# Mixer and passage of a three-stage decoder kernel on one core: conversions ahead of silus, squares and masks, and a norm that starts by token tile

## The chip, the cores and the metric

The kernel runs on one core of a Trainium2 chip. TensorE (PE in the profile) multiplies, VectorE (DVE) and ScalarE (ACT) work on the results, GpSimd (POOL) does a few small operations, and SyncE (SP) issues the loads. The metric is the device time of one execution in microseconds, as the median of several. Lower is better.

## The reference, cut to what matters

Two decoder blocks run one behind the other on 256 tokens of width 1024.

```python
x = x + _moba(_rmsnorm(x, norm_mix), w_qkv, w_o)           # attention, 16 heads
x = x + _conv_ffn(_rmsnorm(x, norm_ffn), w_up, conv, w_down)
x = _rmsnorm(x, norm_final)
h = layer_norm(concat([meta_tokens, x]), ln_emb_g, ln_emb_b)   # 16 + 256 tokens
mix = hybrid_mixer(h, ...)      # gated delta rule (4 heads) and stick-breaking attention
h = layer_norm(ALPHA * h + mix, ln1_g, ln1_b)
h = layer_norm(ALPHA * h + hierarchical_moe(h, ...), ln2_g, ln2_b)   # 32 experts
return h[:, 16:]
```

In the mixer q, k and v of the delta rule pass a causal convolution over 4 tokens and a silu; q and k are normalized by the root of their summed squares; the chunk matrices of q and k are masked, and a triangular system is solved in levels.

## The kernel before

Everything is written by hand in five instruction queues with semaphores; each engine works its own queue strictly in program order.

**Granules.** All weights but the experts' come in granules of 1 MB (128 x 2048), numbered through the program: 0 to 11 for q, k and v, 12 to 15 for the attention's output product (`G_WO` is 12), 16 to 48 for the FFN (`G_FFN` 16), 49 on for the mixer (`G_IN` 49: z, six of q, k and v in the order `DN_ORDER`, six for the other attention, eight gates, and so on). SP loads granule n into one of three buffers `raw` once granule n-3 has been converted (L558). `hi_part` (L744) lets ACT round it to the upper part `whi`, `lo_part` (L1173) lets DVE subtract that from the raw weights and store the rest as `wlo`; there are two slots of each, so granule n also waits for the product with granule n-2. Granules 14 and 48 have slots of their own (`OWN_SLOT`). PE then does three products for each tile (`split3`, L1733): upper by upper, upper by lower, lower by upper. A granule is 48 matmuls of 256 or 272 columns.

```python
def split3(dst, lh, ll, rh, rl, start, stop, **kw):
    pe.matmul(dst, lh, rh, start=start, stop=False, **kw)
    pe.matmul(dst, lh, rl, start=False, stop=False, **kw)
    return pe.matmul(dst, ll, rh, start=False, stop=stop, **kw)
```

**The passage from attention to FFN.** Granules 12 and 13 are multiplied head pair by head pair. Then PE does both token tiles of granule 14 and both of granule 15 (L1868 to L1871); DVE adds each result to the residual `X`; ACT sums the squares of each block of 256 columns (`ss_block`, L823); DVE adds these up, ACT takes the root, DVE takes the reciprocal and scales a tile of 1024 columns to `XN` (`norm_apply`, L1177). PE transposes the tile in 8 pieces (`norm_T`, L1726), ACT writes the upper part (`norm_hi`), DVE the lower (`norm_lo`), and the FFN's first granule waits for all of it. PE fills its waits with products of a row of zeros (`zeros`, L1878, 6, 7 and 7 of them); these also clear the four banks `PM` in which the FFN accumulates. The layer norm of the 16 meta tokens (`MT`, four DVE operations, L1253 to L1258) stands on DVE between granules 14 and 15; its result is first read after the FFN (L1927).

**The mixer's order** is a list `plan` (L208 on) that every engine walks through and takes its own part of: `whole(i)` or `half(i, f)` is PE's product with granule 49+i, and for ACT and DVE the conversion of the granule after it; `out_of(i)` takes the product out of PSUM (ACT a scaled copy, and for q, k and v DVE six tap operations, L1384); `silu`, `square`, `norm`, `G` (chunk matrix of k), `ktr` (k transposed), `QK`, `L0` (first triangular level: POOL masks it, L696, DVE subtracts it from the identity, L1502, PE transposes it, ACT copies it out) are steps of the delta rule. The steps named in `BANKED` share two PSUM banks in turn, in the order of the plan:

```python
TURN[st] = (len(TURN) % 2, len(TURN) // 2)
...
def vacant(eng, *st):
    b, k = TURN[st]
    if k:
        eng.wait_ge(pm_free[b], k)
    return PM[:, b, :]
```

So PE can begin a banked step only when the banked step two places ahead of it has been read out: a `norm` by ACT, a `G` by DVE.

## Time and profile before

| | |
|---|---|
| median of 3 runs | 917.32 us (916.73 to 917.66) |
| the profiled execution, its own time | 919.47 us |
| its span | 917.7 us |
| PE busy | 860.9 us, 94% of the span |
| DVE, ACT, POOL busy | 476.4, 370.0, 61.3 us |
| mean granted clock of TensorE | 0.982 |
| DMA | 193.48 MB, mean 211 GB/s |

The attention takes the first 118 us of the span, the passage 118 to 141, the FFN to 326, the mixer to about 605, the router and the experts the rest. Matmul ends in the profile are modelled: where matmuls follow one another, the distance of their starts tells the pace, not their length.

### The profile page before, as it was taken

How to read it: one execution, taken by the hardware profiler on the slowest of the kernel's cores; microseconds unless marked ns; L12 is line 12 of the kernel's file. 1: busy time of each engine (PE TensorE's matmuls, PEld its weight loads, DVE VectorE, ACT ScalarE, POOL GpSimd, SP SyncE). 2: the span in 40 equal slices, each digit the busy share in tenths (PEclk: the TensorE clock that was granted, in tenths of full speed). 3: DMA queues.
4: the chain of work that ended last, by engine and by line, in shares of the span. 5: the costliest groups of instructions: out<-in, count | busy, mean ns of one | idle time of the engine just before them, and what ended most of it. 6: DMA issues, size and time to landing. Idle time of an engine off the chain costs nothing.

```text
span 917.7 us, 15809 instructions
## 1 busy us (share of the span) xinstructions
PE 860.9 (94%) x6466; PEld 704.0 (77%) x6466; DVE 476.4 (52%) x802; ACT 370.0 (40%) x561; POOL 61.3 (7%) x88
## 2 busy tenths in 40 slices
PE   6999999999999999988999999999899999998882
PEld 6999978989989979988889999998555555544441
DVE  4555675776676786576433355685522322222225
ACT  4655544544555654664435444742211111111111
POOL 0200030000000000001211000003010000000000
PEclk9999997999999999999999999999999999999997
DMA  9854542555555543344122223499599999999991
GB/s 292 287 176 138 177 109 93 184 183 183 183 183 184 184 137 114 116 139 138 47 93 70 71 93 110 166 315 364 213 363 369 364 366 369 364 366 368 366 350 49
DMA packets 151152, 193.48 MB, mean 211 GB/s; under 512 B 4461, under 2 KB 135872, under 8 KB 150960
## 3 DMA queue, kind: packets, MB, share of 16 engines
q1 hardware_dynamic: 148816, 185.61, 60.9%
q0 software_dynamic: 1696, 4.59, 1.6%
q10 hardware_dynamic: 576, 2.36, 0.7%
q8 instruction: 48, 0.79, 0.4%
q14 instruction: 16, 0.13, 0.0%
HBM read 191.50 MB, written 1.05 MB: 210 GB/s over the span
## 4 chain that ended last, share of the span: by engine, by line
PE 74%; DVE 9%; DMA 5%; ACT 5%; SPq 4%; issue 3%; ACTq 0%; DVEq 0%
PE PG L1735 12%; PE PG L1737 12%; PE PG L1736 12%; PE PG L2209 10%; DMA expert_w<-in_expert_w_up 5%; PE PG L2227 4%; PE PM L2236 3%; DVE wlo L1175 3%; SPq L602 2%; PE PM L2063 2%; ACT whi L748 2%; PE PM L1735 2%; PE PM L1737 2%; PE PM L1736 2%; PE PM L2128 1%
## 5 line engine op out<-in xcount | busy, mean ns | idle before, releaser
L1735 PE MATMUL PG<-hT_hi,whi 128*128 128x256 f32 (+1 forms) x832 | 242.1, 291 | 4.6 <-DVE wlo L1175 4.6
L1737 PE MATMUL PG<-hT_hi,wlo 128*128 128x256 f32 (+1 forms) x832 | 237.7, 286 | 0.0
L1736 PE MATMUL PG<-hT_lo,whi 128*128 128x256 f32 (+1 forms) x832 | 237.5, 286 | 0.0
L1175 DVE TENSOR_TENSOR wlo<-raw,whi 128x2048 fp32r<-128x2048 f32 x77 | 177.3, 2302 | 96.4 <-ACT whi L748 96.2
L1735 PEld LDWEIGHTS PG<-hT_hi,whi 128*128 128x128 f32 x832 | 159.8, 192 | 10.5 <-issue 7.9
L1737 PEld LDWEIGHTS PG<-hT_hi,wlo 128*128 128x128 f32 x832 | 159.9, 192 | 0.0
L748 ACT ACTIVATE whi<-raw 128x2048 fp32r<-128x2048 f32 x77 | 146.9, 1908 | 31.4 <-PE PG L1737 26.5
L1736 PEld LDWEIGHTS PG<-hT_lo,whi 128*128 128x128 f32 x832 | 159.3, 191 | 0.1
L2209 PE MATMUL PG<-expert_w,xw 128*64 128x256 f32 x992 | 116.1, 383 | 10.5 <-DMA expert_w<-in_expert_w_up 9.9
L1675 DVE SCALAR_TENSOR_TENSOR y_lo<-PG,small,y_hi 128x512 fp32r<-128x512 f32 x32 | 24.0, 751 | 173.8 <-ACT y_hi L1122 173.8
L2209 PEld LDWEIGHTS PG<-expert_w,xw 128*64 128x64 f32 x992 | 69.4, 137 | 48.9 <-DMA expert_w<-in_expert_w_up 13.3
L2227 PE MATMUL PG<-expert_w,hid 128*64 128x512 f32 x256 | 61.9, 604 | 0.2 <-DMA expert_w<-in_expert_w_down 0.2
L1116 ACT ACTIVATE gusum<-PG 128x256 f32<-128x256 f32 x32 | 12.3, 384 | 119.5 <-PE PG L2209 119.5
L1122 ACT ACTIVATE y_hi<-PG,small 128x512 fp32r<-128x512 f32 x32 | 22.0, 687 | 86.1 <-PE PG L2227 86.1
L2227 PEld LDWEIGHTS PG<-expert_w,hid 128*64 128x64 f32 x256 | 15.6, 136 | 30.0 <-issue 28.2
L1735 PE MATMUL PG<-whi,hT_hi 128*128 128x256 f32 x128 | 36.4, 284 | 1.4 <-DVE hT_lo L1421 0.9
L1737 PE MATMUL PG<-whi,hT_lo 128*128 128x256 f32 x128 | 35.9, 281 | 0.0
L1736 PE MATMUL PG<-wlo,hT_hi 128*128 128x256 f32 x128 | 35.9, 281 | 0.0
L718 POOL COPY xw<-pair 128x512 f32 x31 | 19.1, 615 | 218.4 <-PE PG L2209 200.2
L1735 PE MATMUL PM<-whi,hid_hi 128*128 128x512 f32 x80 | 31.7, 396 | 0.2 <-DVE wlo L1175 0.2
L1793 PE MATMUL PG<-cst 128*128 128x128 f32 (+1 forms) x166 | 27.3, 321 | 4.8 <-DMA cst<-in_consts 4.8
L2236 PE MATMUL PM<-y_hi,hot 64*128 64x512 f32 x128 | 28.8, 444 | 2.9 <-DVE y_lo L1675 2.9
(432 smaller groups left out, 1322.1 us busy)
## 6 DMA issues: line engine op xcount, KB each, us to landing
expert_w<-in_expert_w_gate SPq DMA_DIRECT2D x64, 512.0 KB, 8.9
expert_w<-in_expert_w_up SPq DMA_DIRECT2D x64, 512.0 KB, 10.4
expert_w<-in_expert_w_down SPq DMA_DIRECT2D x32, 1024.0 KB, 10.6
raw<-in_ffn_w_up SPq DMA_DIRECT2D x22, 1024.0 KB, 5.0
raw<-in_w_in SPq DMA_DIRECT2D x22, 1024.0 KB, 5.2
raw<-in_moba_w_qkv SPq DMA_DIRECT2D x12, 1024.0 KB, 6.2
raw<-in_ffn_w_down SPq DMA_DIRECT2D x11, 1024.0 KB, 4.9
raw<-in_moba_w_o SPq DMA_DIRECT2D x4, 1024.0 KB, 5.2
```

The lines of the kernel that those rows point to most:

```text
L718: pool.tensor_copy(xw[i2][:, :, :], pair[:, :, bass.ds(at, WIN)]).then_inc(s_win, 1)
L748: act.activation(hi_of(n), raw[:, n % R, :], ACT.Copy).then_inc(s_hi, 1)
L1122: act.activation(y_hi[:, :], result, ACT.Copy, scale=slotw[i2]).then_inc(s_yhi, 1)
L1175: dve.tensor_tensor(lo_of(n), raw[:, n % R, :], hi_of(n).bitcast(F32), ALU.subtract).then_inc(s_lo, 1)
L1675: dve.scalar_tensor_tensor(y_lo[:, :], result, slotw[i2], y_hi[:, :].bitcast(F32), ALU.mult, ALU.subtract).then_inc(s_y, 1)
L1735: pe.matmul(dst, lh, rh, start=start, stop=False, **kw)
L1736: pe.matmul(dst, lh, rl, start=False, stop=False, **kw)
L1737: return pe.matmul(dst, ll, rh, start=False, stop=stop, **kw)
L1793: pe.matmul(PG[:, 3, 0:x.shape[1]], w, x, start=True, stop=True)
L2209: mm = pe.matmul(PG[WIN * h:WIN * h + WIN, i2, 0:EFF], x[:, KH * kind + k, :], w[:, k, EFF * h:EFF * h + EFF], start=kind + k == 0, stop=k ...
L2227: mm = pe.matmul(result[WIN * h:WIN * h + WIN, :], hid2[i2][:, f, :], w[:, f, 512 * h:512 * h + 512], start=f == 0, stop=f == 1)
L2236: mm = pe.matmul(PM[:, 2 * t + h, :], hot[i2][x, P * t:P * t + P], y[x, :], start=first and y is y_hi, stop=last and y is y_lo)
```

## The change

It has two parts that share nothing but the numbering of own slots.

**In the mixer's plan** the conversion of the next granule goes ahead of silus and squares. `silu` 0 and 1 stand ahead of `out_of(4)` (they read convolutions finished before), `square` 1 and `silu` 2 behind `whole(5)`, `silu_z` and `silu` 3 behind `whole(6)`, `square` 0 and `silu` 4 behind `whole(7)`. `G` 0, 1 and 2 stand ahead of the `norm` pairs that they followed. The subtraction from the identity is a step of its own, `U0`, behind `G` 2; before, DVE did it in `L0`.

**In the passage** granule 15 gets own slots, so it and the FFN's first two granules are converted earlier. PE does tile 0 of granules 14 and 15, then tile 1 of 14, half of tile 1 of 15, the transposes of tile 0, the other half, 12 warming matmuls with the identity, the transposes of tile 1 and 4 zero products. The scaling to `XN` and the waits for it go by halves of 512 columns; the FFN's first granule waits for its input by halves too. The meta tokens' norm goes behind the conversion of granule 17 on DVE.

```diff
-        OWN_SLOT = (14, 48)
+        OWN_SLOT = (14, 15, 48)
...
         whole(4)
-        out_of(4)
         plan_add("silu", 0)
         plan_add("silu", 1)
+        out_of(4)
+        whole(5)
         plan_add("square", 1)
-        whole(5)
+        plan_add("silu", 2)
         out_of(5)
-        plan_add("silu", 2)
         whole(6)
+        plan_add("silu_z")
+        plan_add("silu", 3)
         out_of(6)
-        plan_add("silu", 3)
+        whole(7)
         plan_add("square", 0)
-        plan_add("silu_z")
-        whole(7)
+        plan_add("silu", 4)
         out_of(7)
-        plan_add("silu", 4)
         half(8, 0)
...
         half(9, 0)
+        plan_add("G", 0)
         over("norm", chunks=(0, 1))
-        plan_add("G", 0)
         half(9, 1)
         out_of(9)
+        plan_add("G", 1)
         over("norm", chunks=(2, 3))
-        plan_add("G", 1)
         half(10, 0)
         plan_add("G", 2)
+        plan_add("U0")
         over("ktr", chunks=(0, 1))
...
+            hi_part(G_WO + 3)
...
+            hi_part(G_FFN)
+            for i in range(2):
+                for t in range(TT):
+                    ss_block(t, i, 256 * i, 256 * i + 256, evacs(G_WO + i))
+            hi_part(G_FFN + 1)
+            ss_block(0, 2, D // 2, D, evacs(G_WO + 1) + 2)
+            norm_sqrt(1, [0])
+            ss_block(1, 2, D // 2, 3 * D // 4, evacs(G_WO + 1) + 3)
+            norm_hi(1, [0])
+            ss_block(1, 3, 3 * D // 4, D, evacs(G_WO + 1) + 4)
+            norm_sqrt(1, [1])
+            norm_hi(1, [1])
...
+            dve.wait_ge(s_wo0, 1)
+            dve.tensor_tensor(X[:, 0, D // 2:D], X[:, 0, D // 2:D], PG[:, 2, :], ALU.add).then_inc(s_ev, 2)
+            scale_rows(0)
...
+            norm_lo(1, [0], [0])
+            scale_rows(1)
+            norm_lo(1, [0], [1])
+            norm_lo(1, [1])
...
+            last_rows(G_WO + 2, PG[:, 2, 0:256], 0, 0, KD)
+            last_rows(G_WO + 3, PG[:, 2, 256:512], 0, 0, KD).then_inc(s_wo0, 1)
+            last_rows(G_WO + 2, PM[:, 0, 0:256], 1, 0, KD).then_inc(s_gran, 1)
+            last_rows(G_WO + 3, PG[:, 3, 0:256], 1, 0, KD // 2)
+            pe.wait_ge(s_ev, evacs(G_WO + 1))
+            norm_T(1, 0)
+            last_rows(G_WO + 3, PG[:, 3, 0:256], 1, KD // 2, KD).then_inc(s_gran, 1)
...
+            keep_warm(12, con("ident"), con("ident"), PM[:, 3, :])
+            norm_T(1, 1)
...
+            for b in range(4):
+                pe.matmul(PM[:, b, :], zero[0:1, 0:P], zero[0:1, 0:512], start=True, stop=True)
...
-                features(n, 0, hT_hi, hT_lo, slice(0, SEQ), it)
+                features(n, 0, hT_hi, hT_lo, slice(0, SEQ), it, halves=(s_xlo, 7, 8) if first else None)
```

What it makes of the queues, at the three places that the prediction speaks of. (Lines of the changed file are some ten higher: L750 is `hi_part`, L1174 `lo_part`, L1745 to L1747 `split3`.)

ACT in the mixer, from the product with granule 53 on (`dnT<-PG` copies a product out, `dnT<-dnT` is a silu, `sqb<-dnT` a square, `whi<-raw` the next granule's conversion). Before:

```order
L945 ACTIVATE dnT<-PG,cols 128x272 [waits s_gran]
L945 ACTIVATE dnT<-PG,cols 128x272
L961 ACT_TABLE_LOAD
L961 ACTIVATE dnT<-dnT 128x544 [waits s_ev] x2
L969 ACTIVATE sqb<-dnT 128x1088 [waits s_dnsilu]
L748 ACTIVATE whi<-raw 128x2048 [waits s_gran,landed1]
```

Now:

```order
L960 ACT_TABLE_LOAD
L960 ACTIVATE dnT<-dnT 128x544 [waits s_ev] x2
L944 ACTIVATE dnT<-PG,cols 128x272 [waits s_gran]
L944 ACTIVATE dnT<-PG,cols 128x272
L750 ACTIVATE whi<-raw 128x2048 [waits s_gran,landed1]
L968 ACTIVATE sqb<-dnT 128x1088 [waits s_dnsilu]
L960 ACTIVATE dnT<-dnT 128x544 [waits s_ev]
```

The table load and two silus moved ahead of the copies, the square behind the conversion.

PE in the mixer, between the two halves of granule 58 (`PM<-dnT` is `G` 0, `PM<-sqb,cst` the two `norm` matmuls; pm_free0 and pm_free1 are the two banks). Before:

```order
L1990 MATMUL PM<-sqb,cst 128x272 [waits pm_free0,s_sq]
L1990 MATMUL PM<-sqb,cst 128x272 [waits pm_free1,s_sq]
L2015 MATMUL PM<-dnT 128x128 [waits pm_free0,s_l2]
L2015 MATMUL PM<-dnT 128x128 x3
L1735 MATMUL PG<-hT_hi,whi 128x256 [waits s_lo,s_ev]
```

Now:

```order
L2033 MATMUL PM<-dnT 128x128 [waits pm_free0,s_l2]
L2033 MATMUL PM<-dnT 128x128 x3
L2008 MATMUL PM<-sqb,cst 128x272 [waits pm_free1,s_sq]
L2008 MATMUL PM<-sqb,cst 128x272 [waits pm_free0,s_sq]
L1745 MATMUL PG<-hT_hi,whi 128x256 [waits s_lo,s_ev]
```

`G` 0 moved ahead of both norm matmuls, and the second of them now takes the bank that `G` 0 held. On DVE the conversion of granule 59 stands ahead of the reading of `G` 0 (`dA<-PM`) in both. Before:

```order
L1175 TENSOR_TENSOR wlo<-raw,whi 128x2048 [waits s_hi]
L1435 SCALAR_TENSOR_TENSOR dnT<-dnT,sqb 128x272 [waits pm_free0]
L1435 SCALAR_TENSOR_TENSOR dnT<-dnT,sqb 128x272 [waits pm_free1]
L1477 TENSOR_TENSOR dA<-PM,small 128x512 [waits pm_full0]
L1479 TENSOR_TENSOR dA<-dA,dE 128x512 [waits s_E,s_dve]
```

Now:

```order
L1174 TENSOR_TENSOR wlo<-raw,whi 128x2048 [waits s_hi]
L1486 TENSOR_TENSOR dA<-PM,small 128x512 [waits pm_full0]
L1488 TENSOR_TENSOR dA<-dA,dE 128x512 [waits s_E,s_dve]
L1444 SCALAR_TENSOR_TENSOR dnT<-dnT,sqb 128x272 [waits s_A,pm_free1]
L1444 SCALAR_TENSOR_TENSOR dnT<-dnT,sqb 128x272 [waits pm_free0]
```

The two scalings by a norm moved behind the two operations on `dA`.

PE in the passage, now (`oT` is the attention's result, rows that repeat `split3` left out):

```order
L1745 MATMUL PG<-own_hi_70,oT_hi 128x256 [waits s_lo,s_oTlo]
...
L1745 MATMUL PG<-own_hi_72,oT_hi 128x256 [waits s_lo]
...
L1745 MATMUL PM<-own_hi_70,oT_hi 128x256 [waits s_lo]
...
L1739 MATMUL PG<-cst,XN 128x128 [waits s_xn,s_ev]
...
L1745 MATMUL PG<-own_hi_72,oT_hi 128x256 [waits s_lo]
...
L1805 MATMUL PM<-cst 128x128 [waits s_probT,s_cols]
...
L1739 MATMUL PG<-cst,XN 128x128 [waits s_xn]
...
L1905 MATMUL PM<-zero 128x512 [waits s_zero,s_ev]
```

Before, all four products stood ahead of the first transposes, and 6, 7 and 7 zero products around these.

## Rows read from the trace of the kernel before

**Rows 1.** The page, part 2: TensorE's granted clock in 40 slices, tenths of 2.4 GHz

```profile
PEclk9999997999999999999999999999999999999997
```

**Rows 2.** Windows: length, then busy (x count) per engine, PEclk, DMA share, GB/s

```profile
133.00:134.00 1.00, 1.00 (x7) 0.43 (x6) 0.45 (x3) 0.78 (x4) 0.00 (x0) 0.80 0.92 308
...
146.00:148.00 2.00, 2.00 (x14) 2.00 (x13) 0.00 (x0) 0.00 (x0) 0.00 (x0) 0.69 0.93 381
...
393.00:394.00 1.00, 1.00 (x7) 1.00 (x6) 0.96 (x3) 0.00 (x0) 0.00 (x0) 0.51 0.82 171
...
396.00:397.00 1.00, 1.00 (x9) 1.00 (x8) 0.73 (x1) 0.00 (x0) 0.00 (x0) 0.79 0.35 122
...
444.00:445.00 1.00, 1.00 (x6) 1.00 (x6) 0.00 (x0) 0.18 (x1) 0.79 (x2) 0.60 1.07 382
...
447.00:448.00 1.00, 1.00 (x8) 1.00 (x7) 0.00 (x0) 0.00 (x0) 0.00 (x0) 0.69 0.00 0
```

**Rows 3.** Waits of engine PE: waited for, us in total, times, longest

```profile
PE PG L1735 <- DVE wlo L1175: 5.5, 4, 2.8
```

**Rows 4.** Timeline of PE, passage: start, us, instruction, [idle before]

```profile
117.93 0.36 PE L1735 MATMUL PM<-own_hi,oT_hi 128*128 128x256 f32 x1
...
129.61 1.46 PE L1880 MATMUL PM<-zero 1*128 1x512 bf16 x6
132.31 1.09 PE L1729 MATMUL PG<-cst,XN 128*128 128x128 f32 x8 [1.23 <-DVE XN L1184]
133.33 2.94 PE L1880 MATMUL PM<-zero 1*128 1x512 bf16 x7
...
141.20 0.58 PE L1735 MATMUL PG<-hT_hi,whi 128*128 128x256 f32 x1
...
147.12 0.35 PE L1735 MATMUL PG<-hT_hi,whi 128*128 128x256 f32 x1
```

**Rows 5.** The chain that ended last, warming matmuls at the start

```profile
14.28 3.35 PE PG L1793 x30
```

**Rows 6.** Timelines of DVE and ACT, passage

```profile
129.27 0.40 DVE L1267 TENSOR_TENSOR X<-X,PG 128x256 f32<-128x256 f32 x1
...
130.97 1.28 DVE L1184 SCALAR_TENSOR_TENSOR XN<-X,small,rows 128x1024 f32<-128x1024 f32 x1
...
115.34 1.28 ACT L838 ACT_TABLE_LOAD   x1
```

**Rows 7.** Timeline of PE, mixer

```profile
385.37 0.29 PE L1736 MATMUL PG<-hT_lo,whi 128*128 128x272 f32 x1
...
388.90 0.29 PE L1737 MATMUL PG<-hT_hi,wlo 128*128 128x272 f32 x1
391.98 0.36 PE L1735 MATMUL PG<-hT_hi,whi 128*128 128x272 f32 x1 [2.79 <-DVE wlo L1175]
...
405.55 0.29 PE L1737 MATMUL PG<-hT_hi,wlo 128*128 128x272 f32 x1
...
407.61 0.35 PE L1735 MATMUL PG<-hT_hi,whi 128*128 128x256 f32 x1 [1.77 <-DVE wlo L1175]
...
420.65 0.36 PE L1735 MATMUL PG<-hT_hi,whi 128*128 128x256 f32 x1
...
441.99 1.26 PE L2047 MATMUL PM<-cst,dU 128*128 128x128 f32 x8 [1.20 <-DVE dU L1502]
```

**Rows 8.** Timeline of ACT, mixer

```profile
386.60 1.12 ACT L969 ACTIVATE sqb<-dnT 128x1088 f32<-128x1088 f32 x1
387.61 1.90 ACT L748 ACTIVATE whi<-raw 128x2048 fp32r<-128x2048 f32 x1
```

**Rows 9.** Timeline of DVE, mixer

```profile
383.70 2.78 DVE L1384 SCALAR_TENSOR_TENSOR dnT<-PG,cols,dnT 128x271 f32<-128x271 f32 x6 [2.46 <-ACT dnT L945]
...
418.54 2.29 DVE L1175 TENSOR_TENSOR wlo<-raw,whi 128x2048 fp32r<-128x2048 f32 x1 [1.36 <-ACT whi L748]
...
422.17 0.69 DVE L1479 TENSOR_TENSOR dA<-dA,dE 128x512 f32<-128x512 f32 x1
```

More of the change, by code:

```diff
@@ L746, in hi_part @@
                 if n >= H and n not in own:
-                    act.wait_ge(s_gran, n - H + 1 + 6 * it)
+                    before = max(m for m in range(n) if m % H == n % H and m not in own)
+                    act.wait_ge(s_gran, before + 1 + 6 * it)
                 act.activation(hi_of(n), raw[:, n % R, :], ACT.Copy).then_inc(s_hi, 1)
@@ L1184, in norm_apply, with norm_lo @@
                     dve.scalar_tensor_tensor(XN[:, t, :], X[:, t, :], rs[:, i:i + 1], rows[:, q, :], ALU.mult, ALU.mult).then_inc(s_xn, 1)
-            def norm_lo(q, tiles=range(TT)):
+            def norm_lo(q, tiles=range(TT), parts=range(2)):
                 for t in tiles:
-                    for f in range(2):
+                    for f in parts:
                         dve.wait_ge(s_xhi, 4 * q + 2 * t + f + 1)
@@ L1261, in _ @@
-            for t in range(TT):
-                if t == 0:
-                    dve.wait_ge(s_wo0, 1)
-                else:
-                    dve.wait_ge(s_gran, G_FFN)
-                dve.tensor_tensor(X[:, t, c], X[:, t, c], PG[:, 2 * ((G_FFN - 1) % 2) + t, 0:256], ALU.add).then_inc(s_ev, 1)
-                dve.wait_ge(s_ssq, 3 * TT + t + 1)
-                dve.tensor_reduce(ss[:, 2 + t:3 + t], ssq[:, t, :], AX.X, ALU.add).then_inc(s_ss, 1)
-                norm_apply(1, [t])
-            norm_lo(1)
+                dve.wait_ge(s_gran, n + 1)
@@ new lines, in _, with scale_rows @@
+                dve.tensor_tensor(X[:, :, c], X[:, :, c], PG[:, n % 2, :].rearrange("p (t n) -> p t n", t=TT), ALU.add).then_inc(s_ev, 2)
+            lo_part(G_FFN)
+            def scale_rows(t):
+                i = TT + t
+                dve.wait_ge(s_ssq, 5 if t == 0 else 7)
+                dve.tensor_reduce(ss[:, i:i + 1], ssq[:, t, 0:3 + t], AX.X, ALU.add).then_inc(s_ss, 1)
+                dve.wait_ge(s_rt, i + 1)
+                step(dve.reciprocal(rs[:, i:i + 1], rt[:, i:i + 1]))
+                dve.wait_ge(s_row[1], 16)
+                for f in range(2):
+                    c = slice(512 * f, 512 * f + 512)
+                    dve.scalar_tensor_tensor(XN[:, t, c], X[:, t, c], rs[:, i:i + 1], rows[:, 1, c], ALU.mult, ALU.mult).then_inc(s_xn, 1)
@@ L1309, in _ @@
             lo_part(G_FFN + 1)
+            dve.wait_ge(s_mrt, 1)
+            step(dve.reciprocal(lnrs[0:META, 2:3], lnrt[0:META, 2:3]))
+            step(dve.tensor_scalar(MT[:, :], MT[:, :], lnmv[0:META, 4:5], lnrs[0:META, 2:3], ALU.subtract, ALU.mult))
+            dve.wait_ge(s_row[3], 16)
+            step(dve.tensor_tensor(MT[:, :], MT[:, :], rows[0:META, 3, :], ALU.mult))
+            dve.wait_ge(s_row[0], 16)
+            dve.tensor_tensor(MT[:, :], MT[:, :], rows[0:META, 0, :], ALU.add).then_inc(s_metaln, 1)
             ffn_step(G_FFN, 0, 0, 0, first=True)
@@ L1497, in _ @@
                     dve.tensor_tensor(q, q, ed, ALU.mult).then_inc(s_qd, 1)
-                elif kind == "L0":
-                    c = st[1]
-                    n = CH[c][1]
-                    dve.wait_ge(s_N, MASKED[0, c])
-                    dve.tensor_tensor(mat(dU, cU, c), bc(con("ident")[0:n, 0:n], n, n), mat(dN, cN, c), ALU.subtract).then_inc(s_U0, 1)
+                elif kind == "U0":
+                    for c in range(3):
+                        n = CH[c][1]
+                        dve.wait_ge(s_N, MASKED[0, c])
+                        dve.tensor_tensor(mat(dU, cU, c), bc(con("ident")[0:n, 0:n], n, n), mat(dN, cN, c), ALU.subtract).then_inc(s_U0, 1)
                 elif kind == "Y":
@@ L1740, in w_of, with features @@
                 return (w.rearrange("p (k n) -> p k n", k=k) for w in (hi_of(n), lo_of(n)))
-            def features(n, bank, ah, al, c, it=0, tiles=(0, 1)):
+            def features(n, bank, ah, al, c, it=0, halves=None, tiles=(0, 1)):
                 pe.wait_ge(s_lo, n + 1 + 6 * it)
@@ L1747, in features @@
                     for k in range(KD):
+                        if halves is not None and f == 0 and k % 4 == 0:
+                            pe.wait_ge(halves[0], halves[1 + k // 4])
                         mm = split3(PG[:, bank + f, 0:c.stop - c.start], hw[:, k, P * f:P * f + P], lw[:, k, P * f:P * f + P],
@@ L1788, in tokens_part, with keep_warm @@
                     mm.then_inc(s_gran, 1)
-            def keep_warm(n, w, x):
+            def keep_warm(n, w, x, bank=None):
                 for _ in range(n):
-                    pe.matmul(PG[:, 3, 0:x.shape[1]], w, x, start=True, stop=True)
+                    pe.matmul((PG[:, 3, :] if bank is None else bank)[:, 0:x.shape[1]], w, x, start=True, stop=True)
             pe.wait_ge(s_cst, 16)
```

83 lines of the change are left out of this document (28 added, 55 removed).

## The prediction

> **What bounds the kernel now.** I read the page first: PE is busy 94% of the span, and the granted clock in its 40 slices is 9 tenths or more but for the seventh and the last [rows 1]. PE at full clock is the bound as far as the experts, so there are two things to look for in the two stretches that the change touches: where PE stands still, and where it runs at 1.2 instead of 2.4 GHz. The windows show three low stretches. In the passage the clock falls at 133.8 (0.80 over one us from 133) and is back at 147.2 (0.69 over two from 146): 13.4 us. In the mixer it is low from 393.0 to 396.4 and from 444.2 to 447.6, 3.4 us each [rows 2]. PE's waits by cause put 5.5 us in 4 waits down to the lower parts of weights [rows 3]; two of them, 2.79 and 1.77 us, lie in the mixer [rows 7]. From the FFN's start to its end PE waits for nothing worth a row, and the experts' loads start when the mixer reaches its output product. So what is won in either stretch should move everything behind it, loads too, by as much.
>
> **The passage.** Before: granules 14 and 15 start at 117.93 and are 96 matmuls; the zeros follow at 129.61 [rows 4], so one takes (129.61 - 117.93) / 96 = 0.12 us. Then come six zeros, a wait of 1.23 us for the scaled tile, and transposes, seven zeros, transposes, seven zeros. The FFN starts at 141.20, and its matmuls stand 0.21 us apart (28 up to 147.12) [rows 4].
>
> Now: tile 0 of both granules is 48 matmuls, done at 117.93 + 5.8 = 123.8. From the add to the scaled tile it was 129.27 to 130.97 + 1.28 = 132.25, that is 3.0 us [rows 6]. With an add and a square of 512 columns instead of 256 (0.3 more each, 0.40 having been the time of 256) and with half of the scaling to wait for (0.64 less), the first half is ready at 123.8 + 3.0 + 0.6 - 0.6 = 126.8, the second at 127.5. PE needs them after 84 matmuls, at 128.0: no wait. Eight transposes are 0.93 (1.09 with the last one's tail [rows 4]), the other 12 matmuls 1.4: all products are done at 130.4. From there the second tile's chain to its first half takes 0.25 to reach DVE and 3.0 - 0.6 = 2.4, to 133.1. It is covered by 12 warming matmuls, which the trace counts as 24: at the start of the program 30 such took 3.35 us [rows 5], so these take 2.7, to 133.1. The transposes wait for the second half and end at 134.3; four zeros, 0.22 each at full clock, by six in 1.46 [rows 4], end at 135.2. In the meantime the upper part of the first half (0.6) and its lower part (0.7) are done, at 135.2 too. The FFN starts at 135.25 instead of 141.20: **5.95 us**. If the clock holds, its first 28 matmuls take 28 x 0.12 instead of 5.92: **2.6 us** more.
>
> What had to be early enough for that: granule 15's conversion takes ACT's place at 115.34, where the 1.28 us table load stood [rows 6], and with 1.90 on ACT and 2.29 on DVE [rows 8, 9] it ends at 119.5, needed at 120.8. It pushes the table load, the root and the copy of the columns to 119.1, granule 16 on ACT to 121.0 and 17, behind the squares of blocks 12 and 13, to 124.6: all before the first tile's add and square ask for these engines or right at it. The loads of granules 18 and 19 are issued earlier, since they wait for these conversions. The meta tokens' four operations, three of them over 1024 columns and so about as long as the 1.28 of the scaling [rows 6], start behind granule 17's lower part at 138.1 and end at 142.0. Queued behind them are the taps of the FFN's first product, which PE ends at 141.0 and ACT copies by 142.0: no cost, but no slack. Were PE to start earlier still, this would be what is late next.
>
> **The mixer, first half.** Between granules 53 and 57 ACT did table load (1.28), two silus, and square (1.12) between copying a product out and converting the next granule from 387.61 on [rows 6, 8]; DVE's lower part and PE waited behind them. PE's matmuls of 272 columns stand (388.90 - 385.37) / 28 = 0.126 apart. It should have gone on at 389.03 and did at 391.98: 2.95. It should have gone on at 405.68 and did at 407.61: 1.93. Between, 95 distances take 405.55 - 391.98 = 13.57 where 12.0 are due: 1.6 for the low clock that followed the first wait [rows 2, 7]. Now the chain is the product's copy, the conversion of 1.90, beside it six taps 2.78 from 383.70 to 386.48, and then the lower part 2.29, to 388.8 [rows 8, 9]: 0.2 ahead of 389.03. For granules 56 and 57 it is the same, 0.3 and 0.4 ahead. Gain 2.95 + 1.93 + 1.6 = **6.5 us**, and I count 6.4. The loads are far enough ahead: each is issued when the granule three back is converted, two granules of PE's time before its own turn.
>
> **The mixer, second half.** Here the change adds a wait. The second norm matmul ahead of granule 58's second half needs the bank that `G` 0 now holds. DVE reads `G` 0 only behind the conversion of granule 59, which ran from 418.54 to 420.83, by two operations of 0.69 [rows 9]: in the old time scale the bank is free at 422.25, the norm matmul takes until 422.6, and the half granule that started at 420.65 [rows 7] starts then: 2.0 later. PE stands still for about 3.1 us in one piece, longer than the 2.79 after which the clock fell at 393.0. I take it that the clock falls here too and stays low for 3.4 us, which costs half of it: 1.7. On the other side, `U0` is early, and the wait of 1.20 ahead of the first level's transposes [rows 7] with what follows it (some 0.6) goes: 1.8 back. With that wait goes the low stretch behind it, at 444.2 [rows 2]: half of 3.4, 1.7 back. DVE's reading of `ktr` and `QK` starts about 3 us later behind `U0`; PE reaches them 0.1 to 0.3 late. Sum: -2.0 - 1.7 + 1.8 + 1.7 - 0.1 = **-0.3 us**. The added wait's price is bounded by 0.7 (if `G` 0 is read sooner) and 5.1 (3.4 with the clock's 1.7); I take 3.7, since every term has its row.
>
> **Sum.** 5.95 + 2.6 + 6.4 - 0.3 = 14.65. The profiled execution took 919.47 us, 917.7 of it span; it would come to 904.8, with a span of 903.0. It stood 2.15 above the median of the runs, 917.32, and against that the forecast is **902.7 us**.
>
> **A rule weighed.** In the passage PE ran zeros, transposes and zeros with hardly a gap from 133.33, and the clock stayed at 1.2 GHz to 147.2, 6 us into full matmuls [rows 2, 4]. So products of a row of zeros did not bring it back. The Trainium skill (TensorE: Matmul & The Clock Gate, Part 1: The HAM clock gate) says that the low level is the default and that activity releases it, with no difference made by what the matmuls hold or how many rows they have. By that rule the zeros before should have raised the clock and the four that are left keep it, and the passage's 2.6 us would be certain. The trace disagrees, which leaves the first rival its chance.
>
> **The rivals.**
> - *The clock falls in the passage all the same.* After the warming matmuls there are two short waits, eight transposes and four zeros, 2.1 us of weak work, and in the passage before the fall came behind 0.9 us of zeros, 1.23 of waiting and 1.0 of transposes. Against it: full matmuls now stand directly ahead. It costs the 2.6 and up to 0.5 for zeros at half clock: 905.5. Chance 0.14.
> - *The added wait in the mixer leaves the clock up*, as the one of 1.77 did: 1.7 less, 901.0. Chance 0.12.
> - *The conversions are still late.* The margins of 0.2 to 0.4 us in the mixer's first half are smaller than what one late release takes away; with three waits of up to 1 us each, and the clock falling behind one (1.6), 906.0. Chance 0.10.
> - *No change*, were the experts' loads the bound from a point that does not move. Before 800 us PE hardly waits for them, and they are issued on PE's progress. 917.3, chance 0.02.
> - *Slower: the clock does not recover from the added wait.* In the passage it stayed low for 13.4 us though PE was busy. Behind `G` 0 come granules in halves with small steps and waits between. Each us at the low level costs 0.5; the 14.65 are gone, and 0.2% more, once it has stayed low for 33 us more than the 3.4 counted. If it lasts 40, the time is 921. Against it: both low stretches in the mixer ended after 3.4 us with granules running [rows 2]. Chance 0.03.
>
> **How the numbers follow.** The forecast, 902.7 with 1.5 us either way for terms read a few tenths off, has 0.59. Two in ten may be left out: the range from 900.0 (the second rival and a margin) to 906.5 (the first and the third) leaves out the last two rivals and the tails. About 0.2% is what a measurement of this kernel can tell from no change, 1.8 us. Faster by more is every case but the last two: 0.95; within it 0.02; slower 0.03.
>
> **What would show it.** In the passage the first transposes lie between matmuls of granule 15 without a wait, the FFN starts 17.3 us behind granule 14's start instead of 23.3, at a pace of 0.12. The waits of 2.79 and 1.77 for lower parts are gone. PE waits about 3 us for DVE's `dA` at the norm matmul behind `G` 0, with a low clock of some 3.4 us behind it, and not for `dU` at the first level. The experts are as they were, about 14.6 us earlier. I am wrong if the FFN begins at a pace of 0.21, if a wait for `wlo` is left between granules 53 and 57, if the bank wait is short, or if the meta tokens' norm makes the FFN's first taps late.

## The result, and the profile after

The changed kernel takes **907.33 us** (median of 4, 907.16 to 909.18). Against the kernel before on the same chip the ratio is 0.9897, with a 95% interval of 0.9877 to 0.9916. In a second session, with more executions of both, it was 907.37 us (5) against 919.03 (11), ratio 0.9867, interval 0.9848 to 0.9886. So the change is faster by 1.0 to 1.3%. One more execution of before in the first session took 1687.93 us and is left out of its median. The forecast, 902.7 with 900.0 to 906.5, was 4.6 us too low, and the result lies 0.8 outside its range.

The page's span and its slices of the granted clock (40 slices), after the change:

```profile
span 905.4 us, 15827 instructions
...
PEclk9999999999999999999999999999999999999997
```

The slice that was low before, the seventh [rows 1], is gone. The two profiled executions are 917.7 - 905.4 = 12.3 us of span apart.

**The passage.** PE's timeline from the first transposes to the FFN's first matmul (start, duration, engine, line, operation; a time in brackets would be a wait, and there is none). Left out are granule 15's last 12 matmuls:

```profile
127.98 1.03 PE L1739 MATMUL PG<-cst,XN 128*128 128x128 f32 x8
...
130.29 2.84 PE L1805 MATMUL PM<-cst 128*128 128x128 f32 x24
133.01 1.32 PE L1739 MATMUL PG<-cst,XN 128*128 128x128 f32 x8
134.26 1.03 PE L1905 MATMUL PM<-zero 1*128 1x512 bf16 x4
135.23 0.39 PE L1745 MATMUL PG<-hT_hi,whi 128*128 128x256 f32 x1
```

Every step of PE stands within 0.2 us of its forecast (DVE and ACT end granule 17's conversion and the meta tokens' norm 0.5 to 0.7 us sooner than was worked out); the FFN starts at 135.23, where 135.25 was worked out and 141.20 was before [rows 4]. The windows (busy time of PE, of the weight loads, DVE, ACT and POOL, then the granted clock and the DMA share) show that the clock held, where it had been low for 13.65 us, from 133.60 to 147.25 (the prediction read 133.8 and 13.4 from the windows of [rows 2]):

```profile
130.00:135.00 5.00, 4.99 (x40) 4.07 (x39) 4.00 (x9) 2.00 (x5) 0.00 (x0) 1.00 0.14 18
135.00:148.00 13.00, 13.00 (x110) 12.77 (x109) 10.80 (x14) 5.85 (x8) 0.00 (x0) 1.00 0.26 86
```

**The mixer.** PE's waits by cause (total, times, longest). The waits of 2.79 and 1.77 for `wlo` [rows 3, 7] are gone; in their place two rows wait for DVE's reading of a bank (`L1490`). The first is new. The second, ahead of `ktr`, was 1.45 before:

```profile
PE PM L2008 <- DVEq L1490: 3.8, 2, 2.6
...
PE PM L2044 <- DVEq L1490: 1.8, 1, 1.8
...
PE PG L1745 <- DVE wlo L1174: 1.0, 2, 0.6
```

Before's timeline, ahead of `ktr`:

```profile
431.81 0.63 PE L2026 MATMUL PM<-cst,dnT 128*128 128x128 f32 x4 [1.45 <-DVEq L1481]
```

In order of time (PE's timeline; L2033 is `G`, L2008 `norm`, L2044 `ktr`, L2065 the first level; most matmuls of the granules are left out):

```profile
392.48 0.28 PE L1745 MATMUL PG<-hT_hi,whi 128*128 128x256 f32 x1
...
403.29 1.05 PE L2033 MATMUL PM<-dnT 128*128 128x128 f32 x8
404.18 0.62 PE L2008 MATMUL PM<-sqb,cst 128*128 128x272 f32 x2
407.39 0.70 PE L2008 MATMUL PM<-sqb,cst 128*128 128x272 f32 x2 [2.58 <-DVEq L1490]
407.72 0.48 PE L1745 MATMUL PG<-hT_hi,whi 128*128 128x256 f32 x1
...
413.44 0.70 PE L2008 MATMUL PM<-sqb,cst 128*128 128x272 f32 x2 [1.20 <-DVEq L1490]
...
419.83 1.08 PE L2044 MATMUL PM<-cst,dnT 128*128 128x128 f32 x4 [1.79 <-DVEq L1490]
420.56 0.57 PE L1745 MATMUL PG<-hT_hi,whi 128*128 128x272 f32 x1
...
430.18 1.04 PE L2065 MATMUL PM<-cst,dU 128*128 128x128 f32 x8
```

DVE's own timeline says why: it reads `G` 0 only behind the lower part of granule 59.

```profile
403.57 2.29 DVE L1174 TENSOR_TENSOR wlo<-raw,whi 128x2048 fp32r<-128x2048 f32 x1 [1.36 <-ACT whi L750]
405.78 0.68 DVE L1486 TENSOR_TENSOR dA<-PM,small 128x512 f32<-128x512 f32 x1
406.50 0.69 DVE L1488 TENSOR_TENSOR dA<-dA,dE 128x512 f32<-128x512 f32 x1
```

And the windows of the changed kernel (columns as above), around the two waits and behind the mixer's attention step:

```profile
403.00:408.00 5.00, 2.42 (x17) 1.94 (x17) 4.25 (x4) 1.45 (x3) 0.73 (x1) 1.00 0.19 38
...
420.00:423.00 3.00, 3.00 (x15) 3.00 (x15) 3.00 (x5) 0.00 (x0) 2.31 (x2) 0.50 0.87 262
...
560.00:563.00 3.00, 3.00 (x16) 3.00 (x16) 0.42 (x1) 0.95 (x2) 1.12 (x2) 0.50 1.04 388
```

The clock did not fall behind `G` 0, where I had put it, but at 419.75, as the wait ahead of `ktr` ends, and again at 559.70, 3.4 us each. At the second place PE waits for nothing at all.

**Where the time went.** The same matmul in both traces gives the distance by which the changed kernel is ahead. It is 5.97 at the FFN's start, 8.67 at its end, and 15.13 at granule 57's first half (407.61 and 392.48). At granule 58's second half (420.65 and 407.72) it is 12.93, at the first level (441.99 and 430.18) 11.81, at `vtr` (the transposed v, 448.45 and 434.93) 13.52. Behind the low stretch at 559.7 it is 11.95, and over the whole span 12.3. Up to granule 57 it is ahead of the forecast (14.95); from there on it loses.

### The profile page after: what moved, and what is told of

It is laid out like the page before. It is cut to its first block, busy times and chain, and to the rows that moved or that the text cites. A ratio compares the mean times of both kernels' runs of the same rounds, so it can differ in the third digit from the quotient of the medians.

```text
span 905.4 us, 15827 instructions
## 1 busy us (share of the span) xinstructions
PE 853.0 (94%) x6474; PEld 701.3 (77%) x6474; DVE 477.0 (53%) x804; ACT 369.4 (41%) x559; POOL 61.2 (7%) x88
## 3 DMA queue, kind: packets, MB, share of 16 engines
HBM read 191.50 MB, written 1.05 MB: 213 GB/s over the span
## 4 chain that ended last, share of the span: by engine, by line
PE 74%; DVE 7%; SPq 7%; ACT 5%; DMA 4%; issue 3%; ACTq 0%; DVEq 0%
PE PG L1745 13%; PE PG L1747 12%; PE PG L1746 12%; PE PG L2227 9%; SPq L603 5%; PE PG L2245 4%; DMA expert_w<-in_expert_w_up 3%; PE PM L2254 2%; PE PM L2081 2%; PE PM L1745 2%; PE PM L1747 2%; PE PM L1746 2%; ACT whi L750 2%; SPq L606 2%; PE PM L2146 1%
## 5 line engine op out<-in xcount | busy, mean ns | idle before, releaser
L1745 PE MATMUL PG<-hT_hi,whi 128*128 128x256 f32 (+1 forms) x832 | 240.7, 289 | 0.0
L1747 PE MATMUL PG<-hT_hi,wlo 128*128 128x256 f32 (+1 forms) x832 | 236.1, 284 | 0.0
L1174 DVE TENSOR_TENSOR wlo<-raw,whi 128x2048 fp32r<-128x2048 f32 x76 | 174.1, 2290 | 91.1 <-ACT whi L750 91.0
L1745 PEld LDWEIGHTS PG<-hT_hi,whi 128*128 128x128 f32 x832 | 158.3, 190 | 5.3 <-issue 2.6
L1747 PEld LDWEIGHTS PG<-hT_hi,wlo 128*128 128x128 f32 x832 | 158.5, 190 | 0.0
L750 ACT ACTIVATE whi<-raw 128x2048 fp32r<-128x2048 f32 x76 | 145.1, 1909 | 29.6 <-PE PG L1747 26.7
L1115 ACT ACTIVATE gusum<-PG 128x256 f32<-128x256 f32 x32 | 12.3, 384 | 119.4 <-PE PG L2227 119.4
L1745 PE MATMUL PG<-whi,hT_hi 128*128 128x256 f32 x128 | 36.4, 285 | 1.3 <-DVE hT_lo L1430 0.9
L1747 PE MATMUL PG<-whi,hT_lo 128*128 128x256 f32 x128 | 36.0, 281 | 0.0
L1745 PE MATMUL PM<-whi,hid_hi 128*128 128x512 f32 x80 | 31.6, 395 | 0.2 <-DVE wlo L1174 0.2
```

The source lines that it names most:

```text
L750: act.activation(hi_of(n), raw[:, n % R, :], ACT.Copy).then_inc(s_hi, 1)
L1174: dve.tensor_tensor(lo_of(n), raw[:, n % R, :], hi_of(n).bitcast(F32), ALU.subtract).then_inc(s_lo, 1)
```

## The experiments

The questions: whether the profiled execution of before was a fair base; what the mixer's second half gives back, and to what; and whether the filling matmuls are what held the clock in the passage. Two runs at the end ask what the early `U0` and the new place of the meta tokens' norm are worth. Each comparison with the kernel before is with its executions in the same session.

**The kernel before again.** No edit.

> The kernel before, unchanged, executed again several times. Theory: the profiled execution of before that the forecast was built on (919.47 us) carried low-clock stretches that the median execution does not; each such stretch of 3.4 us costs 1.7 us. Then the spans of the executions scatter by steps of about 1.7 us (915.5 to 918), a longer one has a lower mean clock, and a new trace near the median lacks one stretch that the first had (393.0, 444.2), or has it shorter, at the same waits. Rival: the 2.15 us are something else (a load, the start, the tail); then the low stretches are the same three and the clock's mean does not go with the span.

919.12 us (median of 12, 917.01 to 921.07), beside 17 more executions of before at 919.76 (917.3 to 921.38). The longer an execution, the lower its mean clock: 917.0 at 0.986, 919.1 at 0.982, 920.9 at 0.981. The waits of PE are the same as in the first trace (5.5 us in 4 waits for `wlo`, 1.2 for `dU`), and the clock's low stretches are not:

```profile
134.00:144.00 10.00, 10.00 (x34) 5.63 (x33) 6.32 (x7) 3.98 (x6) 0.00 (x0) 0.51 0.03 10
...
390.00:393.00 3.00, 2.20 (x10) 2.23 (x11) 2.93 (x7) 1.42 (x1) 0.00 (x0) 0.53 0.41 97
407.00:410.00 3.00, 3.00 (x17) 3.00 (x17) 2.96 (x5) 1.88 (x3) 0.00 (x0) 0.54 0.95 290
444.00:447.00 3.00, 3.00 (x25) 3.00 (x26) 0.00 (x0) 0.21 (x1) 0.85 (x2) 1.00 0.66 231
571.00:574.00 3.00, 3.00 (x22) 2.88 (x19) 0.42 (x1) 1.33 (x2) 1.11 (x2) 0.52 0.91 343
```

In the first trace of before the passage was low for 13.65 us and 444 to 447 was low [rows 2], while these two windows were not:

```profile
571.00:574.00 3.00, 3.00 (x28) 2.72 (x28) 0.42 (x1) 1.11 (x3) 0.36 (x1) 1.00 0.71 191
407.00:410.00 3.00, 2.39 (x20) 2.42 (x21) 2.93 (x7) 2.09 (x2) 0.00 (x0) 1.00 0.41 104
```

One program, the same waits, other low stretches. So the theory holds in this: the times scatter with the clock. It fails in the rest: the new trace has one stretch of 3.4 us more, not one less, and its passage is low for 10.24 us instead of 13.65. The low time up to the experts is the same in both, 20.5 us, and so is the time (919.47 and 919.62). The execution of 919.47 was an ordinary one. It was the first three executions (917.32) that were short. The 2.15 us that I took off for the median should not have been taken off.

**The passage alone.** The kernel before with `OWN_SLOT`, the new order in the passage and the meta norm's new place, and the mixer's plan of before.

> The kernel before with the passage's part of the change alone (granule 15 in its own slot, token tile by token tile, the meta norm later); the mixer's plan is before's. Theory: the passage gives 8.67 us, as in the trace of the whole change, and nothing of it depends on the mixer: 917.4 - 8.7 = 908.7, give or take one low-clock stretch of 1.7. The FFN starts at 135.2 at a pace of 0.12; the waits of 2.79 and 1.77 for wlo in the mixer are as before. Rival: the early FFN moves loads onto something later and gives part back; then the offset between the two PE streams, 8.67 at the end of the FFN, shrinks behind it, and the time is 910 or more.

910.10 us (909.81 to 912.55), ratio 0.9906, 0.989 to 0.9922. This execution comes to the passage 0.4 us later than before's and 0.5 later than the changed kernel's (granule 14 at 118.32). From there to the FFN's start it takes 17.40 us, exactly as in the whole change (117.83 to 135.23), and the distance to before is 8.2 at the FFN's end and 8.3 at `ktr`: nothing of it is given back. Behind 448 the distance is 9.8, since the first trace of before is low at 444 and this one is not; the gain of the medians in the same session is 9.7. The waits are before's, and the clock falls at the 2.79 again (at 383.62, just before that wait ends):

```profile
383.00:387.00 4.00, 3.19 (x14) 3.22 (x15) 3.93 (x8) 1.43 (x1) 0.00 (x0) 0.58 0.51 153
```

**The conversions alone.** The kernel before with the first of the plan's two parts:

```diff
         whole(4)
-        out_of(4)
         plan_add("silu", 0)
         plan_add("silu", 1)
+        out_of(4)
+        whole(5)
         plan_add("square", 1)
-        whole(5)
...
-                    act.wait_ge(s_dnsilu, 2 if i == 1 else 4)
+                    act.wait_ge(s_dnsilu, 2 if i == 1 else 5)
```

> The kernel before with one part of the mixer's change alone: silus, squares and masks behind the next granule's conversion; the order of G, norm, U0 and the passage as before. Theory: the two waits for wlo and the low clock behind the first go, 6.4 us, and nothing is given back in the second half: 917.4 - 6.4 = 911.0. The offset to before is 6.4 at granule 57's half and still 6.4 at granule 61's. Rival: what the whole change gave back in the mixer's second half (15.1 at granule 57, 13.5 at granule 61) comes from the conversions' new place, not from G and U0; then it shrinks here too, to 4.8, and the time is 912.6.

912.20 us (911.72 to 913.64), ratio 0.992, 0.9907 to 0.9932. The distance is 6.6 at granule 57's first half and, once the norms behind it are through, 6.2 as far as the first level (441.99 and 435.81); the wait for `wlo` is down to the 1.0 that both kernels have elsewhere. In its session the medians are 7.6 apart, for the 6.4 expected; the profiled execution is the longest of the six (913.64), and its trace ends 5.8 ahead of before's. The 0.4 lost at the norms go with a change in ACT's order: the last silu now stands behind a conversion, 3.5 us after the half granule's start where it was 2.6, the table load follows it, and PE's second pair of norms finds its banks unread. So of the 1.6 that the whole change gave back 0.4 is the conversions', and the rest comes from `G`, `U0` and `ktr`. This trace has no low stretch from 385 to 450, where both traces of before have two, but one at 565, where the first trace of before has none:

```profile
385.00:410.00 25.00, 24.86 (x194) 24.16 (x193) 19.94 (x30) 18.60 (x27) 0.00 (x0) 1.00 0.51 160
410.00:450.00 40.00, 35.29 (x294) 32.39 (x294) 22.09 (x29) 18.17 (x28) 7.58 (x9) 1.00 0.29 91
565.00:569.00 4.00, 4.00 (x28) 3.97 (x25) 0.42 (x1) 1.33 (x2) 1.12 (x2) 0.57 1.04 393
```

**The norms first.** The changed kernel with the order of before at the two banked pairs; `U0` stays early.

```diff
         half(9, 0)
-        plan_add("G", 0)
         over("norm", chunks=(0, 1))
+        plan_add("G", 0)
         half(9, 1)
         out_of(9)
-        plan_add("G", 1)
         over("norm", chunks=(2, 3))
+        plan_add("G", 1)
```

> The changed kernel with the norm pairs ahead of G 0 and G 1 again, as before the change; U0 stays early. Theory: what the change gave back in the mixer's second half is the bank wait: the waits of 2.58 and 1.20 us of the second norm matmul for DVE's reading of G become 0.67 each for ACT (as they were before), 2.4 us less, and the low clock behind them at 419.8 may go too, 1.7 more: 907.3 - 2.4 = 904.9, or 903.2. Rival: DVE is what is late, and PE meets it at the next place whatever the order: then the wait of 1.79 ahead of ktr grows by the 2.4 that the norms no longer wait, and the time stays at 907.

**901.73 us** (901.28 to 903.39), ratio 0.9808, 0.9794 to 0.9822: 5.6 faster than the change. PE's waits in this stretch, and the window over all of it:

```profile
405.15 1.13 PE L2033 MATMUL PM<-dnT 128*128 128x128 f32 x8 [0.68 <-ACT sqb L983]
410.68 1.13 PE L2033 MATMUL PM<-dnT 128*128 128x128 f32 x8 [0.68 <-ACT sqb L983]
417.16 0.63 PE L2044 MATMUL PM<-cst,dnT 128*128 128x128 f32 x4 [1.45 <-DVEq L1490]
```

```profile
380.00:450.00 70.00, 65.61 (x538) 61.86 (x537) 43.23 (x62) 36.82 (x55) 7.59 (x9) 1.00 0.39 121
450.00:620.00 170.00, 164.64 (x1399) 157.57 (x1399) 89.08 (x97) 81.39 (x103) 15.13 (x14) 1.00 0.48 157
```

The wait of 2.58 has become 0.68, that of 1.20 has become 0.68, and the one ahead of `ktr` is shorter, not longer (1.45 against 1.79): the rival is wrong. Both are waits for a bank that one order of two steps brings about. The distance to the changed kernel is 2.2 at granule 59's first half (413.77 and 411.56), 3.0 behind `ktr`, and 4.2 once the changed kernel's low stretch is over. Behind 560, where the changed kernel's trace has another and this one has none, it is 5.8. Of the gain some 2.7 us are waits (2.3 up to `ktr`, 0.3 there); the other 3.1 are the two low stretches, and more than I had expected, since I had not put the stretch at 559 to the account.

**The change again.** No edit.

> The changed kernel, unchanged, executed again beside the kernel before. Theory: of the 4.6 us between forecast (902.7) and result (907.3) one part is the base: the median of before that I subtracted from was low by chance (new executions of before: median 919.1 of 12 and 919.8 of 17), so that against before in one session the gain is about 12.3, as between the two traces: ratio 0.986 to 0.988. A new trace keeps the waits of 2.58, 1.20 and 1.79 us, but may have its low-clock stretches elsewhere. Rival: the ratio stays at 0.990, the gain is 10 in every session; then the trace of before was the exception.

907.37 us against 919.03 in the same session, ratio 0.9867: the expected range. The three waits are the same to 0.04 us (2.62, 1.20, 1.79), and now the clock falls behind both `G` 0 and `ktr`, and not at 559:

```profile
408.00:412.00 4.00, 4.00 (x23) 4.00 (x22) 1.17 (x2) 0.92 (x2) 0.43 (x1) 0.57 0.66 225
...
422.00:425.00 3.00, 3.00 (x15) 3.00 (x15) 3.00 (x5) 0.00 (x0) 2.69 (x3) 0.50 0.94 298
559.00:563.00 4.00, 4.00 (x37) 3.72 (x37) 0.43 (x1) 1.55 (x3) 1.11 (x2) 1.00 0.77 229
```

One of its five executions took 904.81 at a mean clock of 0.993; the others stood at 907.1 to 907.6 and 0.990.

**`G` 2 and `ktr` ahead.** On top of the norms first:

```diff
         plan_add("G", 1)
+        plan_add("G", 2)
         half(10, 0)
-        plan_add("G", 2)
-        plan_add("U0")
         over("ktr", chunks=(0, 1))
+        plan_add("U0")
```

> The version with the norms first (901.73), and in addition G 2 ahead of granule 59's first half and U0 behind ktr. Theory: the wait of 1.45 us of ktr for G 2's bank, which DVE reads only behind the lower part of granule 60, goes, since DVE reads G 2 before that conversion; U0 behind ktr keeps QK from waiting for ktr's banks and is still in time for the first level. 901.7 - 1.4 = 900.3. Rival: DVE is full in this stretch (4.8 of 5 us busy from 415 to 420 in the trace of that version), so PE meets the same lateness at QK or at the first level, and the time stays at 901.7.

901.23 us (900.41 to 902.6), ratio 0.9808, 0.979 to 0.9826. The wait ahead of `ktr` is gone, and one at `QK` has come, for DVE, as the rival had it in part:

```profile
421.53 0.35 PE L2033 MATMUL PM<-dnT 128*16 128x16 f32 x8 [0.54 <-DVE dE L1502]
```

By the traces it is 1.05 ahead of the norms-first version from there to 550, and then loses that to a low stretch from 553 to 557 in this one execution. The medians are 0.5 apart with overlapping intervals; which of the two is better is not settled.

**Zeros for warming.** The changed kernel with one edit:

```diff
-            keep_warm(12, con("ident"), con("ident"), PM[:, 3, :])
+            pe.wait_ge(s_zero, 1)
+            for b in range(12):
+                pe.matmul(PM[:, 3, :], zero[0:1, 0:P], zero[0:1, 0:512], start=True, stop=True)
             norm_T(1, 1)
```

> The changed kernel with 12 zero matmuls of one row, 0.22 us each at full clock, in place of the 12 warming matmuls of 128 rows in the passage. Theory (the forecast's first rival): what keeps the clock up is that the filling matmuls work on all 128 rows; with zeros, PE does about 5.5 us of one-row products and transposes, the clock falls near 133 and stays low into the FFN: the FFN starts up to 1.5 later at a pace of 0.21, and the time is 907.3 + 3 to 5 = 910 to 912. Rival: any matmul counts as activity; then the clock stays at 1.00 from 130 to 148 and the time is 907.3.

909.49 us (908.91 to 913.52), 2.1 above the change in the same session. PE's timeline and windows:

```profile
130.74 2.76 PE L1902 MATMUL PM<-zero 1*128 1x512 bf16 x12
133.43 1.72 PE L1739 MATMUL PG<-cst,XN 128*128 128x128 f32 x8
135.08 1.88 PE L1907 MATMUL PM<-zero 1*128 1x512 bf16 x4
136.89 0.58 PE L1745 MATMUL PG<-hT_hi,whi 128*128 128x256 f32 x1
```

```profile
134.00:140.00 6.00, 6.00 (x23) 4.24 (x23) 5.39 (x7) 1.19 (x2) 0.00 (x0) 0.50 0.02 7
```

The 12 zeros take as long as the warming did (2.76 and 2.84), PE is busy throughout, and the clock falls at 134 and is back at 140.8. The four zeros behind take 1.88 instead of 1.03, and the FFN starts at half pace, 18.70 us behind granule 14's start (118.19) where it was 17.40. The theory is right in its cause. By the traces the passage loses 3.1 us, as expected (3.4 from 145 on, of which 0.4 stood there before the passage). The medians are only 2.1 apart. In this trace the mixer has one low stretch where the change's has two, and behind 565 the distance is down to 1.9; whether the other executions are like it, no trace shows.

**Before with warming.** The kernel before, its 20 one-row zeros each replaced:

```diff
-                    pe.matmul(PM[:, b % 4, :], zero[0:1, 0:P], zero[0:1, 0:512], start=True, stop=True)
+                    pe.matmul(PM[:, b % 4, 0:P], con("ident"), con("ident"), start=True, stop=True)
```

> The kernel before with its 20 zero matmuls of one row in the passage replaced by 20 of the 128 rows of the identity, which take as long at full clock. Theory: the clock stays up through the old passage too (it fell for 10 to 13.6 us in the traces of before), although the wait of 1.23 us for the scaled tile is still there: the FFN starts at a pace of 0.12, 1.5 to 2 us sooner, and with its first stretch at full clock the gain is 5 to 6.5 us: 913 to 914. Rival: it is the waits for the scaled tiles that let the clock fall, whatever PE does between; then it falls again near 133, and at most it recovers sooner: 917 to 919.

913.19 us (911.23 to 915.15) against 919.03, ratio 0.994, 0.992 to 0.996. The old passage, with its wait of 1.29 us and all its steps:

```profile
132.65 1.09 PE L1729 MATMUL PG<-cst,XN 128*128 128x128 f32 x8 [1.29 <-DVE XN L1184]
...
138.23 0.39 PE L1735 MATMUL PG<-hT_hi,whi 128*128 128x256 f32 x1
```

```profile
130.00:138.00 8.00, 6.45 (x57) 6.08 (x55) 5.88 (x12) 4.32 (x11) 0.00 (x0) 1.00 0.44 133
```

The clock stays up though PE is busy only 6.45 of 8 us, and the FFN starts at 138.23 instead of 141.20 [rows 4]. So 5.8 us of the passage's 9.7 (by the medians; 5.6 of 8.2 between the traces at the FFN's end) come with the filler alone. This kernel is a measurement and not one to use: the FFN adds its products to what is in the four banks, and the matmuls put in write the identity to 128 of the 512 columns of each, so it leaves out the clearing that the zeros did. The change does that with its four zeros behind the warming. The two experiments go from either side to the same place: what filled PE's gap decided the clock, and not the wait. In the 12 traces of this study the passage is low in the four kernels' traces with one-row fillers alone (before twice, the conversions alone, zeros for warming) and in none of the eight with warming matmuls. The two kinds of filler differ in rows (1 and 128), in type (bf16 and fp32) and in columns (512 and 128); which of these counts was not tried.

**`U0` back in its place,** on top of the norms first, so that of the mixer's part only the conversions are left.

> The version with the norms first (901.73), and U0 back in its old place, so that of the mixer's change only the conversions are left. Theory: U0's early place is worth the wait of 1.20 us ahead of the first level and the small ones behind it, 1.35 in the two traces' offsets: 901.7 + 1.4 = 903.1, up to 904.8 where a low-clock stretch follows the wait as it did in two traces of before (at 444). Rival: the early U0 only moves DVE's load, and ktr and QK pay for it: then 901.7.

904.59 us (903.47 to 905.25), ratio 0.984, 0.9824 to 0.9856, 2.9 above. The wait for `dU` is back, and the clock stays up behind it this time:

```profile
427.29 1.26 PE L2064 MATMUL PM<-cst,dU 128*128 128x128 f32 x8 [1.20 <-DVE dU L1510]
```

The distance between the two traces is 1.3 at the first level, 1.5 from there to the experts and 2.0 at the end. The rest of the 2.9 is not in these two traces. `U0` early pays for itself.

**The meta norm early,** on top of the norms first: the four operations ahead of the first tile's add on DVE.

> The version with the norms first (901.73), and the meta tokens' four operations on DVE back in the passage, ahead of the first tile's add. Theory: they take 3.7 us there (0.14, 0.80, 1.22, 1.22 and the gaps) from 123.0 on, so the add that began at 123.93 begins at 126.7, the first transposes follow 2.8 later than their products, and PE stands still for about 1.9 us behind its last product before the warming matmuls, with both tiles' chains 2.8 late: the FFN starts at 137.5 to 138 instead of 135.2; 904.2, or 906 and more if the clock falls there. Rival: DVE's gaps in the passage (0.92, 0.79, 2.62 us) take them in; then it stays at 901.7.

905.23 us (903.92 to 905.75), ratio 0.9844, 0.9827 to 0.9861, 3.5 above. DVE and PE:

```profile
126.90 0.67 DVE L1269 TENSOR_TENSOR X<-X,PG 128x512 f32<-128x512 f32 x1
```

```profile
129.97 1.23 PE L1739 MATMUL PG<-cst,XN 128*128 128x128 f32 x8 [1.73 <-DVE XN L1266]
...
137.41 0.39 PE L1745 MATMUL PG<-hT_hi,whi 128*128 128x256 f32 x1
```

The add that began at 123.93 begins at 126.90, PE waits 1.73 for the scaled tile, and the FFN starts at 137.41, 2.1 later. The clock holds through it. The other 1.5 us of this trace are a low stretch at 557, which the norms-first trace does not have; so some 2.1 of the 3.5 are shown to be the norm's. The new place behind granule 17's lower part is part of the gain, and costs nothing there: in the changed kernel the four operations run from 137.81 to 141.29, and the taps wait 0.58 for ACT, not for them.

## Why the prediction missed

Of the 4.6 us, 2.15 are a step that should not have been taken (the base, taken from three executions), 1.55 a low stretch of the clock that was not in the sum, and 1.3 the mixer's second half, where two waits were not followed; small terms give 0.5 back, and the median stands 0.2 above the profiled execution.

**The passage was right, step by step**: 5.97 for the forecast's 5.95 at the FFN's start, and 8.67 for 8.55 with the clock. The second number holds for the trace of before that the forecast was built on: against before's second trace, whose passage was low for 3.4 us less, it is 7.5. The trace of zeros alone had spoken against a rule, and I had kept 0.14 for a fall; the two exchanges show that the warming matmuls are what holds the clock, and that four zeros behind them do no harm. The Trainium skill (TensorE: Matmul & The Clock Gate, Part 1: The HAM clock gate) has activity release the low level and names no difference between kinds of matmuls; these traces show one between the two fillers, at nearly the same busy time of PE (2.76 and 2.84 us).

**The mixer's first half was right**: 6.46 (15.13 - 8.67) for 6.4. The conversions arrive in time, and the third rival is wrong.

**The mixer's second half was the step that failed: -1.6 in place of -0.3.** Its terms, from the same distances:
- The wait for `G` 0's bank cost 1.9 (14.72 to 12.81) for the 2.0 forecast: right. PE stood still for 2.58 where about 3.1 was forecast.
- The same wait at `G` 1 was left out. It is 1.20 where 0.67 stood, and costs 0.5 (12.81 to 12.32). `ktr`, where DVE is now late by 1.79 for 1.45 and which I had put at 0.1 with `QK`, costs 0.3 (to 11.98). I had followed the bank at the first pair and not at the second. The row was there to be read: the order of the change repeats the exchange.
- The pair of norms ahead of granule 58 lost 0.4 (15.16 to 14.72 at 414.97 and 400.25), which I did not have either: the same loss stands in the trace of the conversions alone.
- The early `U0` brought 1.4 at the first level (10.45 to 11.81) and 0.2 with what follows: I had 1.8. The separate runs give 1.5.
- The low clock, where I booked 1.7 lost behind `G` 0 and 1.7 won back at 444, came at `ktr` instead, for 1.5 (11.98 to 10.45), and went as booked at 444, for 1.5 (12.03 to 13.53). The sum came out nearly right, and the reason did not: see below. Here too the trace of before counts: against its second trace, low at 407 and not at 444, the distance is 15.3 at 413.5 and 12.1 behind 448, so that the second half gives back 3.3 there.

**A term that I did not have: 1.55 us at 559.7.** The clock fell in the changed kernel's profiled execution where PE was busy with products of 16 columns and the attention's, and waited for nothing. No edit touches that stretch. In the 12 traces of this study that stretch has a low clock in 5 (the change, before again, conversions alone, `G` 2 ahead, the meta norm early) and none in 7. The changed kernel's own two traces differ in it. Whether it comes is decided by the execution, not by the change.

**The base: 2.15 us.** I worked the sum against a trace of 919.47 and then took off what that trace stood above the median of three runs. 49 more executions, with medians of 919.0 to 920.0 by session, say that it was the three runs that stood low, each within the range of the 49 or 0.2 below it. Without that step the forecast would have been 904.8, and with the same room around it (2.7 below, 3.8 above) would have held the result.

Together: 14.65 forecast, +0.1 in the passage, +0.1 in the first half, -1.3 in the second, -1.55 at 559.7, and +0.3 at the tail: 12.3, the difference of the two spans.

**What is wrong with booking the clock by place.** I gave each low stretch to a wait and moved it with the wait. The same waits in other traces, with falls that begin inside the wait or up to 2.2 us behind its end:
- Behind the 2.79 for `wlo` the clock fell in 4 of 4 (before twice, the passage alone, before with warming).
- Behind the 2.6 for `G` 0's bank it fell in 2 of 3 (not in the change's first trace).
- Behind the 1.79 ahead of `ktr` it fell in 2 of 3, and behind the 1.45 that stands there in eight other traces in none.
- Behind the 1.77 for `wlo` it fell in 1 of 4 (before again, at 407.26). I had leaned on this wait as one that leaves the clock up.
- Behind the 1.20 for `dU` it fell in 1 of 6: the one on which I had booked a gain of 1.7.

So the longer wait was the likelier one: 6 of 7 for those over 2.5 us, 3 of 7 for those near 1.8, 1 of 17 for these of 1.2 and 1.45 and the 1.20 at `G` 1 (0 of 3). All 12 traces also have a wait of 1.4 us near 330 and one of 1.5 near 640, and none of these 24 has a fall. Which fall belongs to which wait is read from their nearness; it was not tested.

A fall is a chance that a wait carries and not a part of it. The same section of the Trainium skill says that the monitor runs freely and does not start with the kernel, so that the number of slow matmuls at a kernel's start differs from run to run; these traces show the places of the falls in the middle of a program differ from run to run too. Had I weighed that, the -1.7 and +1.7 would have been shares of 1.7 each, and the range would have had 1.7 either way for the clock alone. It also would have told me that the added wait was dear: the changed kernel's two bank waits come with 4 falls in 6 chances, some 2.3 us on average, beside the 2.7 us that the waits cost. The norms first takes that away, 5.0 together, and its median is lower by 5.6.

The slower rival, a clock that does not recover, did not occur: every fall in the mixer ended after 3.4 us. No time near 917 was seen.

## What to carry to other kernels

Where two steps that share rotating banks change places, follow the bank at every later pair and not only at the first, and ask behind which long operation its reader is queued. Fill a gap of the matmul engine with matmuls like those of the work, here 128 rows in fp32: one-row bf16 fillers kept it as busy and let its clock fall, 2.1 us in one direction and 5.8 in the other. A low clock behind a wait is a chance per execution; count how often it comes in several traces before it is booked, and take the base from more executions than three, and the ledger of distances from more than one trace of before.

## What the hardware did that I had not expected

- One program shows its low-clock stretches at other places in each execution, at waits that agree to 0.04 us. The times of the kernel before go from 916.9 to 921.4 and follow its mean clock (0.986 to 0.980).
- The clock can fall while PE waits for nothing: at 559.7 in the changed kernel, in a stretch with a busy share of 1.00, behind products of 16 columns.
- A gap does not have to cost the clock: with warming matmuls around it, a wait of 1.29 us and PE busy 6.45 of 8 us left it at 1.00.
- `tensor_scalar` over 16 rows of 1024 took 0.80 us in its new place and 1.26 in its old one, in every trace looked at (four and five), while an operation of the same size with two tensors took 1.21 to 1.22 at both. No run says why.
